# Two-layer MoE decoder on one core: the router worked out by token halves, and the gather by pieces

## The chip, the cores and the metric

The kernel runs on one core of a Trainium2 chip. The metric is the device time of one execution in microseconds (us), measured outside the profiler: 1168.0 us is the median of three runs (1166.81, 1168.00 and 1169.35). Everything is float32. One hardware DMA queue, driven by SyncE (SP), brings in all weights. TensorE (PE), VectorE (DVE) and ScalarE (ACT) compute; GpSimd clears one tile at the start and does nothing more.

## The reference, cut to what matters

256 tokens of width 1024 go through two layers. Each layer is a mixer (retention and HGRN2 in the first; stick-breaking and differential attention in the second) with an output projection, and then a hierarchical mixture of experts: every token picks one group of four by its group logits, and in that group the two best of eight experts, so that two of 32 experts work on it.

```python
x = x + mix.astype(x.dtype)                 # mixer with its output projection
h = rms_norm(x, norm_ffn[l])                # one scale per token, one gain per column
g_logits = hf @ wg_r + bg_r                 # 4 groups
g_sel = argmax(g_logits);  p_g = softmax(g_logits)[g_sel]
e_in  = (hf @ we_r + be_r)[group g_sel]     # 8 experts of that group
top_v, top_i = top_k(e_in, 2)
gate = p_g * softmax(top_v)
a = silu(xb @ w_gate[e]) * (xb @ w_up[e]);  y = a @ w_down[e]
out = segment_sum(y_rows * gate)            # and x = x + out
```

Every layer reads the gate, up and down matrices of all 32 experts, 2 MB each, 96 of them.

## The kernel before, in words

**Weights and places.** A unit is one 2 MB matrix, 128 partitions by 4096 numbers. SBUF holds twelve places for units (`RING + WIDE`); the mixer's input blocks, its two output blocks and the experts' 96 units pass through them in a fixed order. SP issues each load as soon as the unit that lay in its place before has been used; the counter `unit_used` (raised by the last matmul that reads a unit) says so. Experts go by quads of four: the units of a quad are four gate matrices, four up, four down. While the mixer still runs, SP loads the first quad (units 0 to 11 of the layer) into places as they come free. The last two of these are held back: unit 5 goes to the place of the second output block, so it waits for the last matmul of the output projection; unit 6 lies where the turned tokens and the router's weights are, and waits for the router's `strips`. Unit 12 needs the place of unit 0, so it waits for the first expert matmuls. Unit 0 of the first quad is cut by rows (`QUARTERED`): units 0 to 3 hold rows 0 to 255, 256 to 511 and so on of all four gate matrices, so that after row chunks 0 and 1 (of eight) unit 0 is used up, after 2 and 3 unit 1, and so on. Units 16 to 83 come by fours in one transfer (`load_matrices`, L391).

**Output projection and router** (`project_out` L1109, `route_and_experts` L1140 on PE; `finish_mixer` on ACT L1364 and on DVE L1540; `route` L1582 on DVE). The tokens are two halves of 128. PE finishes half 0, then the first 512 columns of half 1, turns the eight blocks of x of half 0 (`turn_x`, 128 by 128 transposes), does two matmuls for the second 512 columns of half 1, turns four more blocks, and does the last two matmuls. The last of them raises `unit_used`. Then come the router's strips for half 0 (`strips`: eight matmuls of 64 rows, two chunks side by side in the array), the last four blocks of x, the strips of half 1 and the `logits` matmuls that add the two strips. DVE adds the mixer's sums into x, copies the strips of half 0, and works out the inverse root mean square of both halves after all squares (ACT makes Ln and Exp, DVE refines with four operations). Then `route` takes both halves at once: scores (L1602), 640 differences of pairs (L1605), their comparison (L1606), their sum (L1608), the chosen group (L1609), the picked experts (L1611). PE counts ranks (L1170 to L1174), DVE writes the rank table (L1617) and the selection matrix `sel` (slots of 32 tokens for each of four experts: a comparison, L793, and a multiplication with the tokens' scales, L799). PE gathers the tokens by matmuls with `sel` (L577), ACT multiplies by the gains on the way to `xT` (L743), and the gate matmuls (L631) begin with the first two chunks. Between these PE writes x into the sum banks (`start_sums`, L558) and does two filler matmuls (`keep_busy`, L553).

**The quads.** For each quad: gate, up, gather of the next quad, four transposes, down, spreading back. ACT makes the sigmoid, DVE the product. `lbt`, `consts` and the like are small tables.

**Order.** All of it is written out by hand: each engine runs its own list in order, and waits on counters. Nothing reorders it.

## Time and profile before

| what | value |
|---|---|
| median of three runs | 1168.0 us |
| the profiled execution's own time | 1166.55 us |
| its span | 1164.8 us |
| PE busy | 876.4 us (75%) |
| DVE busy | 223.8 us (19%) |
| ACT busy | 126.7 us (11%) |
| bytes moved | 447.45 MB, 384 GB/s on the mean |
| mean granted TensorE clock | 0.877 |

The page of the profile cuts the span into 40 slices of 29.1 us; a digit is a busy share in tenths. The router stages lie in slices 6 and 26, at about 157 to 183 us and 722 to 748 us. The view of windows gives busy times of the engines in stretches that one chooses, and last the granted clock, the share and the speed of the DMA engines. The timeline gives start, length, engine, line, operation, tiles and shapes, and behind "x" how many instructions are merged in a row; a float32 matmul is two instructions. "SPq" is SyncE's issue of a transfer, not the transfer.

### The profile page before, as it was taken

What the parts mean: (1) busy time and instruction counts of PE and PEld (TensorE: products, weight loads), DVE (VectorE), ACT (ScalarE), POOL (GpSimd) and SP (SyncE); (2) the same over time, 40 slices, a digit from 0 to 9 for tenths busy, and PEclk for the clock granted to TensorE, in tenths of its full rate; (3) what the DMA queues carried; (4) which work ended last, traced back from release to release, by engine and by line L of the source; (5) the groups of instructions that cost most, each with busy time, mean ns of one, the idle gap of its engine ahead of it and who ended that gap; (6) DMA issues with size and microseconds to landing.
All of it is one profiled execution on the core that took longest, in us unless ns stands there. A gap on an engine that the chain in (4) does not pass through costs nothing.

```text
span 1164.8 us, 11459 instructions
## 1 busy us (share of the span) xinstructions
PE 876.4 (75%) x5104; PEld 394.0 (34%) x5104; DVE 223.8 (19%) x470; ACT 126.7 (11%) x249; POOL 0.5 (0%) x5
## 2 busy tenths in 40 slices
PE   8999999747474738485899999977474747474776
PEld 7555554212121212121246655433131313131312
DVE  2732332010101010101127541410000101000001
ACT  3411311000000000000021431200000000000000
POOL 0000000000000000000000000000000000000000
PEclk9999999888888877777999999998787878788889
DMA  9776659999999999999996477899999999999997
GB/s 347 304 321 257 267 219 378 430 435 433 435 433 433 435 433 435 435 430 414 424 423 284 154 293 276 317 441 433 433 435 435 433 435 433 433 430 432 417 426 308
DMA packets 19637, 447.45 MB, mean 384 GB/s; under 512 B 2560, under 2 KB 2816, under 8 KB 5504
## 3 DMA queue, kind: packets, MB, share of 16 engines
q1 hardware_dynamic: 19584, 446.67, 91.0%
q8 instruction: 43, 0.70, 0.2%
q14 instruction: 10, 0.08, 0.0%
HBM read 445.61 MB, written 1.05 MB: 383 GB/s over the span
## 4 chain that ended last, share of the span: by engine, by line
DMA 56%; PE 42%; DVE 1%; another core or an unknown queue 1%; issue 0%; ACT 0%; SPq 0%; DVEq 0%
DMA places<-in_together 47%; PE psum L631 14%; PE psum L1016 11%; DMA places<-in_quarters 8%; PE psum L1117 5%; PE psum L1013 4%; PE psum L577 1%; PE psum L1029 1%; PE psum L1057 1%; PE psum L565 1%; DMA places<-in_w_in 0%; PE psum L1144 0%; PE psum L698 0%; PE psum L968 0%
## 5 line engine op out<-in xcount | busy, mean ns | idle before, releaser
L631 PE MATMUL psum<-places,mixed 128*32 128x512 f32 x3040 | 421.8, 707 | 276.3 <-DMA places<-in_together 249.2
L631 PEld LDWEIGHTS psum<-places,mixed 128*32 128x32 f32 x3040 | 110.4, 127 | 570.5 <-issue 448.7
L1016 PE MATMUL psum<-places 128*128 128x512 f32 x288 | 126.3, 593 | 0.0
L1016 PEld LDWEIGHTS psum<-places 128*128 128x128 f32 x288 | 53.6, 190 | 61.4 <-issue 61.2
L577 PEld LDWEIGHTS psum<-sel,x 128*128 128x128 f32 x528 | 60.4, 192 | 17.0 <-issue 15.1
L577 PE MATMUL psum<-sel,x 128*128 128x128 f32 x528 | 64.3, 279 | 1.7 <-DVE sel L799 1.7
L565 PE MATMUL psum<-y_sb,spread 128*128 128x512 f32 x128 | 59.6, 606 | 2.1 <-ACT y_sb L768 1.4
L820 DVE TENSOR_TENSOR sig<-psum,sig 128x512 f32<-128x512 f32 x16 | 11.1, 692 | 253.4 <-ACT sig L760 253.4
L823 DVE TENSOR_TENSOR mixed<-psum,sig 128x512 f32<-128x512 f32 x16 | 11.1, 692 | 245.4 <-PE psum L631 245.4
L833 DVE COPY y_sb<-psum 128x512 f32<-128x512 f32 x14 | 9.7, 692 | 180.2 <-PE psum L631 180.2
L762 ACT COPY mixed<-psum 128x512 f32<-128x512 f32 x16 | 9.4, 586 | 320.6 <-PE psum L675 320.6
L1013 PE MATMUL psum<-places 128*128 128x256 f32 x192 | 42.9, 381 | 0.0
L1013 PEld LDWEIGHTS psum<-places 128*128 128x128 f32 x192 | 36.1, 190 | 5.7 <-issue 1.0
L760 ACT ACTIVATE sig<-psum 128x512 f32<-128x512 f32 x16 | 9.6, 597 | 255.9 <-PE psum L631 255.9
L565 PEld LDWEIGHTS psum<-y_sb,spread 128*128 128x128 f32 x128 | 22.8, 189 | 38.6 <-issue 33.7
L768 ACT COPY y_sb<-psum 128x512 f32<-128x512 f32 x16 | 9.4, 586 | 209.2 <-PE psum L631 181.8
L1117 PE MATMUL psum<-places,y_sb 128*128 128x512 f32 x64 | 28.2, 594 | 0.7 <-ACT small L1396 0.7
L1117 PE MATMUL psum<-places 128*128 128x512 f32 x64 | 28.5, 592 | 0.0
L826 DVE TENSOR_TENSOR mixed<-psum,consts 128x512 f32<-128x512 f32 x32 | 21.9, 690 | 31.8 <-PE psum L577 31.8
L1117 PEld LDWEIGHTS psum<-places,y_sb 128*128 128x128 f32 x64 | 11.9, 190 | 14.8 <-issue 13.9
L1388 ACT ACTIVATE places<-psum,small 128x512 f32<-128x512 f32 x16 | 10.1, 684 | 57.7 <-PE psum L1016 53.6
L1117 PEld LDWEIGHTS psum<-places 128*128 128x128 f32 x64 | 11.8, 190 | 13.4 <-issue 13.4
(252 smaller groups left out, 505.4 us busy)
## 6 DMA issues: line engine op xcount, KB each, us to landing
places<-in_singles SPq DMA_DIRECT2D x32, 2048.0 KB, 10.1
places<-in_quarters SPq DMA_DIRECT2D x22, 2048.0 KB, 35.1
places<-in_w_in SPq DMA_DIRECT2D x12, 2048.0 KB, 26.7
places<-in_w_out SPq DMA_DIRECT2D x4, 2048.0 KB, 14.3
places<-in_quarters SPq DMA_DIRECT2D x4, 1024.0 KB, 45.6
places<-in_w_in SPq DMA_DIRECT2D x2, 1024.0 KB, 27.2
places<-in_w_in SPq DMA_DIRECT2D x3, 512.0 KB, 8.7
x<-in_x SPq DMA_DIRECT2D x2, 512.0 KB, 13.6
```

The lines of the kernel that those rows point to most:

```text
L565: mm = pe.matmul(psum[:, ACC + 2 * n + tc, :], spread[:, tc, :], y_sb[:, 512 * n:512 * (n + 1)], start=False, stop=False, skip_group_check ...
L577: mm = pe.matmul(psum[:, YB + c // 4 if bank is None else bank, (c % 4) * P:(c % 4 + 1) * P], x[:, tc, c * P:(c + 1) * P], sel[:, tc, :], ...
L631: mm = pe.matmul(psum[slots, out + n, :], inp[:, c, slots], slot(layer, unit)[:, at + 512 * n:at + 512 * (n + 1)], start=c == 0, stop=c == ...
L820: turn(nc.vector.tensor_tensor(sig, psum[:, GATE, :], sig, ALU.mult))
L823: nc.vector.tensor_tensor(flat(act_h), psum[:, UP, :], sig, ALU.mult).then_inc(m["act_ready"], 1)
L826: nc.vector.tensor_tensor(xT[:, 4 * half:4 * half + 4, :], psum[:, 6 + half, :].rearrange("p (c s) -> p c s", s=P), gain_cols[:, 2 + layer ...
L1013: mm = pe.matmul(banks[:, m // 2, (m % 2) * SEQ:(m % 2 + 1) * SEQ], w[:, c, m * P:(m + 1) * P], hT[:, c, :], start=c == 0, stop=c == KC - 1)
L1016: mm = pe.matmul(banks[:, m, :], hT[:, c, m * P:(m + 1) * P], w[:, c, :], start=c == 0, stop=c == KC - 1)
L1029: mm = pe.matmul(psum[:, 4 + m, 0:SEQ], w[:, c, m * P:(m + 1) * P], hT[:, c, :], start=c == 0, stop=c == KC - 1)
L1057: mm = pe.matmul(banks[:, m, :], hT[:, c, m * P:(m + 1) * P], w[:, c, :], start=c == 0, stop=c == KC - 1)
L1117: return pe.matmul(psum[:, OUT_BANK[layer] + 2 * tc + n, :], mixT(half)[:, c, tc * P:(tc + 1) * P], w[:, c, 512 * n:512 * (n + 1)], start= ...
L1388: r = nc.scalar.activation(dst[:, tc * 512:(tc + 1) * 512], proj(g)[:, tc, :], function, scale=small[:, 2 + tc:3 + tc])
```

## The change

The diff computes the same in another order and in smaller pieces.

- `project_out` takes in the strips of half 0 ahead of the last-but-one output matmul, and the logits of half 0 ahead of the last one.
- Each half has a root of its own (`ask_root`, `refine_root`, `mean_square`); ACT takes the first after the turned half 0 is copied.
- `route` works by half: scores, differences, picks and ranks of half 0, then of half 1. The addition of the last 512 columns to x (`finish_x`) stands behind the differences of half 0.
- `sel` is 0 or 1 without the scales. The scale of each slot comes from one narrow matmul (`scale_slots`) and a copy by ACT (`keep_scale`), and enters in the sigmoid, in the product with it and in that with the up result, for every quad.
- The first gather goes by chunks: one, one, two, two, two, each between gate matmuls (`begin_gather`, `go_on_gathering`); the counts for the overflow test come in the midst of it. The gate values' exponentials and the load of the sigmoid's table come behind the gather, `start_sums` for three of four banks between the gate and the up matrices, and the read of the count into PE's register after the last gate matrix.

```diff
-ROOTS = ((2, 2), (20, 8), (28, 8), (2, 2), (2, 2), (44, 16), (44, 16), (44, 8), (2, 2))
+ROOTS = ((2, 2), (20, 8), (28, 8), (2, 1), (3, 1), (2, 2), (44, 16), (44, 16), (44, 8), (2, 1), (3, 1))
...
+            def scale_slots(bank):
+                for tc in range(TC):
+                    mm = pe.matmul(psum[:, bank, SEQ:SEQ + 1], sel[:, tc, :], small[:, 2 + tc:3 + tc], start=tc == 0, stop=tc == TC - 1)
+                return mm
+            def begin_gather():
+                pe.wait_ge(S["sel_first"], layer + 1)
+                gather_some(0, 1, YB + 1, (0,))
+                gather_some(1, 2, YB, (0,))
+                pe.wait_ge(m["sel_ready"], 1)
+                gather_some(0, 1, YB + 1, (1,)).then_inc(S["gather_begun"], 1)
+                gather_some(1, 2, YB, (1,))
+                scale_slots(YB).then_inc(S["gather_begun"], 1)
+            def go_on_gathering(c):
+                begun = 3 * layer
+                if c == 0:
+                    pe.wait_ge(S["xT_begun"], begun + 1)
+                elif c == 1:
+                    pe.wait_ge(S["xT_begun"], begun + 2)
+                elif c == 2:
+                    gather_some(2, 4, YB + 1, range(TC)).then_inc(m["gathered"], 1)
+                    count_picked(pe)
+                    pe.wait_ge(m["xT_ready"], 1)
+                elif c == 3:
+                    gather_some(4, 6, YB, range(TC)).then_inc(S["gather_begun"], 1)
+                elif c == 4:
+                    pe.wait_ge(S["xT_begun"], begun + 3)
+                elif c == 5:
+                    gather_some(6, 8, YB + 1, range(TC)).then_inc(m["gathered"], 1)
+                elif c == 6:
+                    pe.wait_ge(m["xT_ready"], 2)
...
                 if first:
-                    pe.wait_ge(S["xT_begun"], layer + 1)
+                    matrix(0, 0, GATE, xT, KC, FF, each_chunk=go_on_gathering)
+                    start_sums(pe, layer, (1, 2, 3))
+                    pe.wait_ge(S["route_ready"], layer + 1)
...
-                nc.scalar.activation(sig, psum[:, GATE, :], ACT.Sigmoid).then_inc(m["sig_ready"], 1)
+                nc.scalar.activation(sig, psum[:, GATE, :], ACT.Sigmoid, scale=slot_scale).then_inc(m["sig_ready"], 1)
...
             def one_hots(quad):
-                placed(sel, quad)
-                nc.vector.tensor_tensor(sel, sel, small[:, 2:4].unsqueeze(2).broadcast_to([P, TC, P]),
-                                        ALU.mult).then_inc(m["sel_ready"], 1)
+                placed(sel, quad).then_inc(m["sel_ready"], 1)
...
                         turn_x(pe, layer, 1, 0)
-                        for c in range(2, 4):
-                            mm = out(1, c, 1)
+                        pe.wait_ge(S["router_ready"], layer + 1)
+                        pe.wait_ge(S["xT_first"], layer + 1)
+                        strips(layer, 0, range(KC)).then_inc(S["strips"], 1)
+                        out(1, 2, 1)
+                        pe.wait_ge(S["strips_kept"], layer + 1)
+                        logits(0).then_inc(S["logits_done"], 1)
+                        mm = out(1, 3, 1)
                     mm.then_inc(S["unit_used"], 1)
...
+                pe.wait_ge(S["xT_second"], layer + 1)
+                strips(layer, 1, range(KC // 2))
                 turn_x(pe, layer, 1, 1)
                 pe.wait_ge(S["xT_third"], layer + 1)
-                strips(1, range(KC // 2, KC)).then_inc(S["strips"], 1)
-                start_sums(pe, layer, (0,))
+                strips(layer, 1, range(KC // 2, KC)).then_inc(S["strips"], 1)
                 pe.wait_ge(S["last_strips_kept"], layer + 1)
                 logits(1).then_inc(S["logits_done"], 1)
-                start_sums(pe, layer, (1, 2, 3)).then_inc(S["sums_started"], 1)
-                keep_busy(pe, 2, 7, ident, consts[:, 0:SEQ])
+                pe.wait_ge(S["picked_ready"], TC * layer + 1)
+                pe.matmul(psum[:, 4, 0:32], before, picked[:, 0, :], start=True, stop=True).then_inc(S["ranks_done"], 1)
+                start_sums(pe, layer, (0,))
+                pe.wait_ge(S["scores_read"], layer + 1)
+                pe.matmul(psum[:, 5, 0:32], ones[:, 0:P], picked[:, 0, :], start=True, stop=False)
+                keep_busy(pe, 2, 7, ident, consts[:, 0:SEQ])
+                pe.wait_ge(S["picked_ready"], TC * layer + 2)
+                pe.matmul(psum[:, 5, 0:32], before, picked[:, 1, :], start=False, stop=True).then_inc(S["ranks_done"], 1)
...
+                dve.wait_ge(S["squares"], SQUARES[2 * layer] + 2)
+                scores(0)
+                differences(0)
+                finish_x(layer)
+                pick(0)
+                dve.wait_ge(S["squares"], SQUARES[2 * layer + 1])
+                turn(V.tensor_tensor(small[:, 1:2], small[:, 1:2], small[:, 7:8], ALU.add))
+                ask_root(mean_square(dve, layer, 1), 3, 1)
+                refine_root(dve, turn)
+                scores(1)
+                V.memset(small[:, 60:61], 0.0).then_inc(S["scores_read"], 1)
+                differences(1)
+                pick(1)
+                place_first(0).then_inc(S["sel_first"], 1)
+                place_first(1).then_inc(M[layer]["sel_ready"], 1)
```

## Rows read from the trace of the kernel before

**Rows 1.** The page: DMA share by slice, GB/s by slice, and the chain's shares.
```profile
DMA  9776659999999999999996477899999999999997
GB/s 347 304 321 257 267 219 378 430 435 433 435 433 433 435 433 435 435 430 414 424 423 284 154 293 276 317 441 433 433 435 435 433 435 433 433 430 432 417 426 308
...
DMA 56%; PE 42%; DVE 1%; another core or an unknown queue 1%; issue 0%; ACT 0%; SPq 0%; DVEq 0%
```

**Rows 2.** Windows around both routers; the last column is GB/s.
```profile
156.50:164.50 8.00, 8.00 (x30) 3.90 (x28) 1.99 (x4) 3.37 (x6) 0.00 (x0) 1.00 0.00 0
164.60:176.50 11.90, 10.93 (x80) 7.60 (x84) 7.94 (x27) 2.51 (x8) 0.00 (x0) 1.00 0.90 352
176.50:179.00 2.50, 2.50 (x23) 1.06 (x23) 1.46 (x9) 2.10 (x5) 0.00 (x0) 1.00 0.02 7
179.00:184.00 5.00, 5.00 (x49) 2.35 (x51) 2.03 (x6) 1.15 (x4) 0.00 (x0) 1.00 0.95 331
729.70:741.30 11.60, 10.62 (x75) 7.41 (x76) 7.94 (x27) 2.38 (x8) 0.00 (x0) 1.00 0.92 362
743.60:754.00 10.40, 10.40 (x96) 4.33 (x100) 3.20 (x10) 1.96 (x6) 0.00 (x0) 1.00 0.91 356
```

**Rows 3.** Timeline of SP's issues: units 5, 12, 16 to 19; layer 1: 5, 12.
```profile
164.59 0.33 SPq L369 DMA_DIRECT2D places<-in_singles  x1
...
178.42 0.33 SPq L369 DMA_DIRECT2D places<-in_singles  x1
...
192.63 0.33 SPq L391 DMA_DIRECT2D places<-in_together  x1
...
729.73 0.33 SPq L369 DMA_DIRECT2D places<-in_singles  x1
...
743.57 0.33 SPq L369 DMA_DIRECT2D places<-in_singles  x1
```

**Rows 4.** Timeline of the first router, from the output projection's end to the sums.
```profile
160.72 1.01 ACT L974 COPY places<-psum 128x1024 f32<-128x1024 f32 x1 [1.90 <-PE psum L968]
...
162.67 1.88 PE L1117 MATMUL psum<-places 128*128 128x512 f32 x4
...
164.49 1.09 PE L1144 MATMUL psum<-places 128*64 128x128 f32 x16
164.59 0.69 DVE L1551 TENSOR_TENSOR x<-x,psum 128x512 f32<-128x512 f32 x1 [4.06 <-PE psum L1117]
...
166.69 0.21 ACT L866 ACTIVATE small<-small 128x2 f32<-128x2 f32 x1
...
168.58 0.31 PE L1149 MATMUL psum<-both_strips,mixed 128*128 128x40 f32 x2
...
168.72 2.82 PE L558 MATMUL psum<-x,consts 128*128 128x512 f32 x6
```

**Rows 5.** The same timeline, from the pairs to the first gate matmuls.
```profile
169.46 0.82 DVE L1605 TENSOR_TENSOR mixed<-mixed 128x640 f32<-128x640 f32 x1
...
172.03 0.17 DVE L1609 TENSOR_SCALAR mixed<-mixed 128x8 f32<-128x8 f32 x1
172.24 0.23 DVE L1611 SCALAR_TENSOR_TENSOR picked<-mixed 128x64 f32<-128x64 f32 x1
...
172.52 0.43 PE L1170 MATMUL psum<-picked,consts 128*128 128x64 f32 x2
...
173.97 0.42 DVE L799 TENSOR_TENSOR sel<-sel,small 128x256 f32<-128x256 f32 x1
...
174.45 2.05 PE L577 MATMUL psum<-sel,x 128*128 128x128 f32 x16 [0.86 <-DVE sel L799]
...
175.65 0.63 ACT L743 ACTIVATE mixed<-psum,consts 128x128 f32<-128x128 f32 x2 [7.65 <-PE psum L577]
...
176.44 1.92 PE L631 MATMUL psum<-places,mixed 128*32 128x512 f32 x16
...
177.38 1.28 ACT L1383 ACT_TABLE_LOAD   x1
```

More of the change, by code:

```diff
@@ L711, in moe_pe @@
             y_all = 2 * QUADS
+            count = pe.value_load(over_i[0:1, layer:layer + 1], min_val=0, max_val=SEQ)
             with pe.If(count > SLOTS):
@@ L771, in act_quad @@
                     nc.scalar.copy(y_sb[:, 512:1024], psum[:, YB + 1, :]).then_inc(m["y_ready"], 1)
-            keep_gathered(n17 + 1, first=not over)
+            if over:
+                keep_gathered(n17 + 1)
+            else:
+                begin_gathered()
             with act.Fori(0, QUADS if over else QUADS - 1) as i:
@@ L1107, in turn_half, with strips, logits @@
                 turn_mixed(pe, layer, half)
+            def strips(layer, tc, chunks):
+                for c in chunks:
+                    at = 64 * (c % 2)
+                    mm = pe.matmul(psum[at:at + 64, 4 + tc, 0:P], rw[layer][:, c, :], hT[:, c, tc * P:(tc + 1) * P],
+                                   start=c < 2, stop=c >= KC - 2)
+                return mm
+            def logits(tc):
+                return pe.matmul(psum[:, 4 + tc, SEQ:SEQ + SCORES], by_logit[:, tc * P:(tc + 1) * P], both_strips,
+                                 start=True, stop=True)
             def project_out(layer, meanwhile):
@@ L1640, in gates @@
                 V.tensor_reduce(rt[:, 8:10], differ, AX, ALU.add).then_inc(S["top_diff"], 1)
+                largest_count(layer)
                 dve.wait_ge(S["group_exp"], layer + 1)
```

204 lines of the change are left out of this document (101 added, 103 removed).

## The prediction

> **What bounds the kernel now.** I read the page first. Its slices show two kinds of stretch [rows 1]: the expert stages run at 430 to 435 GB/s with the DMA share at 9 for 13 or so slices each, and the mixers (slices 0 to 5, 21 to 25) move 154 to 347 GB/s. The chain gives 56% to DMA and 42% to PE [rows 1]. So the mixers go at PE's pace, the expert stages at the transfers' pace, and a stage with experts ends a fixed number of bytes after its stream starts: what moves that start moves the end by as much, twice in the kernel.
>
> So I looked next, by windows, at where the stream really starts. From 156.5 to 164.5 nothing moves [rows 2], since all free places are filled. At 164.59 SP issues unit 5, the release being the last output matmul; unit 6 follows behind the strips, while 5 is under way [rows 3]. From 164.6 to 176.5 the two are moved: 11.9 x 352 = 4.19 MB, which is 9.7 us at 433 GB/s. They were over by about 176.1 (11.6 x 362 = 4.20 MB by 741.3 in layer 1), so an issue into an idle queue costs 176.1 - 164.6 - 9.7 = 1.8 us before the stream counts as full. Then comes a hole: 7 GB/s from 176.5 to 179.0 [rows 2]. Unit 12 is issued at 178.42 [rows 3], when row chunks 0 and 1 of the gate are done. From 179 to 184 only 5 x 331 = 1.66 MB move, 3.8 us at full speed, so the stream counts as full from 180.2, again 1.8 us after the issue. The hole is worth 180.2 - 176.1 = 4.1 us. In layer 1 the issue is at 743.57 and 10.4 x 356 = 3.70 MB are 8.55 us of full speed by 754.0: full from 745.45, unit 6 over at 741.2, hole 4.2 us.
>
> Two events set the start of the endless stream, then: A, the release of unit 5 (the last output matmul), after which 11.5 us of transfer follow; and B, the release of unit 12 (gate chunk 1). Before, B is the late one. Full speed from then on is the later of A + 11.5 and B + 1.8. The change pulls B ahead and pushes A back.
>
> **A, the output projection's tail.** Strips of half 0 are 16 instructions, 1.09 us with the array's run-out and 1.02 from start to start; logits two instructions, 0.31 us [rows 4]. Both now stand ahead of the last output matmul. Strips wait for the copy of turned half 0, done at 160.72 + 1.01 = 161.73 [rows 4], and PE gets to them at 162.84 (the start of the last four output instructions, 162.67, plus array time): no wait. Then an output matmul of two instructions (4 take 1.72 us between starts, so 0.86) to 164.72. Logits need DVE's copy of the strips (128 wide; 0.29 us by the fixed part and slope worked out below), which stands behind the root: ACT's Ln and Exp (0.21 each [rows 4]) after the copy, 161.73 + 0.45, then four dependent small operations of 0.17 with 0.04 between them [rows 5], to 163.0. Strips end at 163.86, the copy at 164.2, half a microsecond ahead of need. So A moves by 1.02 + 0.35 = 1.4 us, to 166.0. If the root came later than that, it would delay A one for one (rival 3). Unit 6 needs the strips of half 1, now at about 169.1; unit 5 is under way until 172.6, so this is hidden. A + 11.5 = 177.5.
>
> **B, the chain to the second gate chunk.** DVE, in order: scores of half 0 at 165.2; differences of 320 instead of 640 elements. 640 cost 0.82 and 64 cost 0.23 [rows 5], a slope of 1.02 ns and a fixed 0.16, so 320 cost 0.49. By the slope alone it would be 0.33, by the whole row 0.82, and I keep these as ends. To 165.95. Then the addition to x, 0.69 us [rows 4], after A, to 166.75. Picks of half 0: 0.49 + 0.49 + 0.17 + 0.20 and gaps: to 168.25. ACT's squares of the last 512 columns end at 167.6, so the second root starts at 168.25: sum, mean, Ln, Exp, four refinements, some 1.7 us: 169.95. Beside it PE turns the last four blocks once x is added (166.95 to 167.5), ACT copies them to 168.25 behind its squares, PE does four strips to 169.05, ACT keeps them to 169.4, logits stand at 169.95. Both arms meet; scores of half 1 at 170.0. Then 0.21, a marker of 0.1, 0.49, 0.49, 0.49, 0.17, 0.20 with gaps: picked at 172.35. Before it was 172.24 + 0.23 = 172.47 [rows 5]: the splitting by itself gives next to nothing here, because A moved and each fixed cost is paid twice.
>
> What is won comes after. Ranks are one matmul instead of four (0.43 for two instructions [rows 5], the others were beside); rank table and `sel` of half 0 (0.20 + 0.29) run while PE does the ranks of half 1; then 0.20 + 0.29 for half 1, and no multiplication of `sel` (0.42 [rows 5]): `sel` ready at 173.55 against 173.97 + 0.42 = 174.4. Next PE needs two more gather instructions before ACT may start, not eight: 16 take 2.05 [rows 5], so 0.26 for 2; with the handover of 0.15 seen before ACT's row (eight at 174.45 + 0.99, ACT at 175.65), ACT starts at 174.0. One chunk costs it 0.31 (half of 0.63 [rows 5]), PE begins the gate at 174.45 where it was 176.44, and chunk 1 is ready before chunk 0 ends (0.86 to 0.93, an eighth of the 16 instructions' 1.92 by fours [rows 5]). B = 174.45 + 2 x 0.87 = 176.2, where it was 178.42: 2.2 us earlier. B + 1.8 = 178.0.
>
> **The sum for one layer.** Full speed from the later of 177.5 and 178.0, before 180.2: 2.2 us. But at 176.2 the queue is still busy with unit 6, and an issue into a busy queue may be spared part of the 1.8 us; the trace shows no such late join, so between 0 and 0.5 us more. I take 0.2: 2.4 us a layer, bounds 2.2 and 2.7. Layer 1 has the same order and nearly the same times from A on (13.84 us from A to B against 13.83 [rows 3]): 4.8 us for both.
>
> The 1.8 us are read from the front of a transfer: 7 GB/s until 179.0, 0.6 us after the issue, then 331 GB/s over five microseconds [rows 2]. The Trainium skill says otherwise: its page "DMA: Bandwidth & Descriptors", section "Anatomy of one DMA — SWDGE (gpsimd) path", puts most of a fixed cost of about 2 us behind the last byte, as the write's receipt. What that would make of the time is rival (2); the rows do not bear it out for this queue.
>
> **What else is moved.** The remaining gathers now stand between gate chunks: two chunks' gather 0.99 and counting 0.4 ahead of chunk 2, and ACT's two chunks: chunk 3 ends at 180.9, which releases unit 13. Unit 12 lasts to 178.0 + 4.84 = 182.8; an issue is wanted 1.8 before that, at 181.0. It just fits. The gate ends at 185.5. Then three sums, 6 instructions, 2.6 us of PE (2.82 with run-out [rows 4]), which were formerly under DVE's picking, and up's 6.9: the up units are used at 195.1 where it was 192.63 [rows 3]. Units 12 to 15 last until 178.0 + 19.35 = 197.35; wanted by 195.55. It fits by 0.5 us. If that cover is gone, each microsecond of PE costs one. ACT's exponentials and table load (some 1.7 us) now end at about 185.3, beside the gate; the weights of `selw` are wanted 10 us later. The read of the count before the branch in the last quad stands where PE waits for transfers anyway. In each of the 16 quads there come four narrow matmul instructions and a small copy (0.6 us together by the 0.17 and 0.43 us rows), and 0.42 of DVE goes. The three products with an added per-slot scalar keep their 512 elements; ends are no change and 0.1 us each. All of this lies where PE waits for transfers, and 0.6 us before the last quad's down matrix, whose last quarters come some 12 us later. I count 0.
>
> **The time.** The profiled execution took 1166.55 with a span of 1164.8; minus 4.8 it would be 1161.75 and 1160.0. It lies 1.45 under the median, so for the median 1168.0 - 4.8 = 1163.2 us.
>
> **Rivals.** (1) The sums and gathers that moved behind the gate eat the cover of 0.5 us: if up's release is 1.5 us later than worked out, the first transfer of four comes 1.0 too late in each layer: 1165.2. For it: three separate PE to ACT handovers in the gate. Against it: those rows are all short.
> (2) The slow start is no lost time, made up by the sixteen engines later: then the hole is only 176.1 to 178.5 (unit 12's issue), and after the change full speed runs from 177.5, a gain of 1.0 us a layer: 1166.0. For it: 433 GB/s is a mean over units in flight together. Against it: the 331 GB/s. It is what would follow from the page named above.
> (3) Slower: the hold of the output projection. Unit 5 is queued behind PE's wait for the copied strips, that behind DVE's root, that behind ACT's Ln and Exp. It costs from the first 0.5 us of lateness on and turns the gain into a loss when A moves by more than 180.2 - 11.5 - 164.6 = 4.1 us, that is when logits stand 2.7 us later than worked out. One load of an activation table there (1.28 us [rows 5]) would make A + 2.2, still faster. With logits 3.6 us late, as when ACT's pair is served only after the squares and the copies of half 1 (some 4 us of its list), it is A + 5.0: 1168.0 + 2 x 0.9 = 1169.8. For it: three engines in a ring at a place where before there was no wait. Against it: ACT is free from 161.73 on.
> (4) B comes late, because the second half's chain on DVE (18 dependent operations) costs 0.1 more at each: B = 178.0, 0.4 a layer, 1167.2.
>
> **How the numbers follow.** Forecast 0.58, with its own range 1161.5 to 1164.8 (bounds 2.2 and 2.7 a layer, give or take 1.2 us of the median seen in three runs); (1) 0.14; (2) 0.06; (3) 0.09; (4) 0.13. 0.2% is 2.3 us, about what a measurement of this kernel can tell from no change. Faster takes the forecast, (1) but for a few hundredths, and a share of (2) and (4): 0.57 + 0.11 + 0.04 = 0.72. Same: the rest of those, 0.19. Slower: (3), 0.09. The range is 1160.8 to 1167.6.
>
> **What would show it.** In the profile after: unit 5's issue 3.1 us after the strips' start, where it stood at their start; unit 12's issue 10.2 us behind unit 5's, not 13.8; no window near 0 GB/s between unit 6 and unit 12, nor before the first transfer of four. The forecast is wrong if a hole remains, if logits of half 0 wait for DVE, or if the first transfer of four is issued into an empty queue.

## The result, and the profile after

| | median us | range us | runs |
|---|---|---|---|
| before | 1168.07 | 1166.41 to 1169.35 | 18 |
| after | 1170.62 | 1167.13 to 1172.03 | 18 |

The ratio is 1.0018, 95% interval 1.0011 to 1.0026: some 2 us slower, where 4.8 us faster was forecast. The profiled execution of after took 1171.11 us with a span of 1169.3 (before: 1166.55 and 1164.8) at the same mean granted clock of 0.877. PE's program grew from 5104 matmul records to 5180.

The page of after, against [rows 1]: DMA and GB/s by slice, the queue that brings instructions, the chain's shares. In the slices of the experts nothing is gained. The instruction queue moved 45 packets (before: 43 and 0.70 MB). PE's share of the chain rose by 3 points, and "issue" from 0% to 1%.

```profile
DMA  9776659999999999999996476899999999999996
GB/s 346 301 284 275 254 194 421 431 431 435 431 431 433 431 435 431 435 433 411 424 422 279 154 295 271 335 446 433 430 434 430 434 437 432 430 435 433 415 425 266
...
q8 instruction: 45, 0.74, 0.3%
...
DMA 51%; PE 45%; another core or an unknown queue 1%; DVE 1%; issue 1%; ACT 1%; SPq 0%; DVEq 0%
```

SP's issues of units 5, 12 and 13 and the first transfer of four, against [rows 3]:

```profile
168.83 0.33 SPq L370 DMA_DIRECT2D places<-in_singles  x1
...
178.91 0.33 SPq L370 DMA_DIRECT2D places<-in_singles  x1
...
183.87 0.33 SPq L370 DMA_DIRECT2D places<-in_singles  x1
...
198.38 0.33 SPq L392 DMA_DIRECT2D places<-in_together  x1
```

All of this stands 2.8 us late, for a reason that has nothing to do with the change: the first projection took 16.87 us in this execution and 14.05 in that of before (last section). So from here on times are also given from a mark. "From unit 4" is the distance from unit 4's issue, which stands at 149.54 in before and 152.34 in after; "from the output block" is the distance from the issue of layer 1's output block (611.15 and 613.60).

| from unit 4's issue | before | after | moved | forecast |
|---|---|---|---|---|
| A: unit 5 issued | 15.05 | 16.49 | +1.44 | +1.4 |
| B: unit 12 issued | 28.88 | 26.57 | -2.31 | -2.2 |
| unit 13 issued | 32.72 | 31.53 | -1.19 | just in time |
| first transfer of four issued | 43.09 | 46.04 | +2.95 | just in time |
| layer 1's output block issued | 461.61 | 461.26 | -0.35 | -2.4 |

Layer 1, from the output block: A 118.58 to 120.02, B 132.42 to 130.10, unit 13 136.26 to 135.06, the first transfer of four 146.64 to 149.57. The last copy of the kernel starts at 550.47 before, 552.57 after: +2.10.

Windows over after's router, against [rows 2]; the last column is GB/s. The hole of 7 GB/s is gone, as forecast. In its place come six microseconds at 339.

```profile
176.50:179.00 2.50, 2.50 (x24) 1.04 (x23) 0.75 (x4) 0.76 (x3) 0.00 (x0) 1.00 0.99 426
179.00:181.00 2.00, 1.65 (x16) 1.35 (x19) 0.34 (x2) 0.63 (x2) 0.00 (x0) 1.00 1.06 369
181.00:184.00 3.00, 3.00 (x28) 1.36 (x24) 0.00 (x0) 0.63 (x2) 0.00 (x0) 1.00 0.86 339
184.00:187.00 3.00, 3.00 (x29) 1.36 (x25) 0.33 (x2) 1.19 (x5) 0.00 (x0) 1.00 0.89 339
187.00:190.00 3.00, 3.00 (x20) 1.12 (x13) 2.75 (x12) 1.59 (x2) 0.00 (x0) 1.00 0.97 388
```

The timeline of the router (start, length, engine, line, operation, tiles, shapes; "x" counts merged instructions), against [rows 4, 5]:

```profile
165.57 1.09 PE L1171 MATMUL psum<-places 128*64 128x128 f32 x16
...
168.27 0.49 DVE L1675 TENSOR_TENSOR mixed<-mixed 128x320 f32<-128x320 f32 x1
...
174.68 0.19 DVE L1686 SCALAR_TENSOR_TENSOR picked<-mixed 128x32 f32<-128x32 f32 x1
...
175.60 0.29 DVE L1693 TENSOR_TENSOR sel<-consts,rank 128x128 f32<-128x128 f32 x1
...
176.93 1.92 PE L668 MATMUL psum<-places,mixed 128*32 128x512 f32 x16
```

Less 2.8, `picked` is ready at 172.07 (forecast 172.35), `sel` at 173.09 (173.55), the gate begins at 174.13 (174.45). The router does what was said of it.

The last quad of layer 1 does not do what was said of it. PE's matmuls of its up matrices (the first two rows) and of its down matrices in after:

```profile
1133.69 1.07 PE L668 MATMUL psum<-places,mixed 128*32 128x512 f32 x8 [0.34 <-issue]
1139.56 7.55 PE L668 MATMUL psum<-places,mixed 128*32 128x512 f32 x56 [4.81 <-issue]
1150.28 1.92 PE L668 MATMUL psum<-places,mixed 128*32 128x512 f32 x16 [1.01 <-ACT spread L814]
1153.63 1.92 PE L668 MATMUL psum<-places,mixed 128*32 128x512 f32 x16
1156.97 1.92 PE L668 MATMUL psum<-places,mixed 128*32 128x512 f32 x16
1158.71 1.04 PE L732 MATMUL psum<-places,mixed 128*32 128x512 f32 x8
...
1166.17 0.69 DVE L892 COPY x<-psum 128x512 f32<-128x512 f32 x1 [0.17 <-PE psum L566]
```

and in before (up matrices, again the first two rows, then the first of the down matrices, and the end):

```profile
1129.94 5.36 PE L631 MATMUL psum<-places,mixed 128*32 128x512 f32 x48
1136.98 1.92 PE L631 MATMUL psum<-places,mixed 128*32 128x512 f32 x16 [1.68 <-DMA places<-in_quarters]
1141.97 1.92 PE L631 MATMUL psum<-places,mixed 128*32 128x512 f32 x16 [1.30 <-DMA places<-in_quarters]
...
1154.14 1.07 PE L698 MATMUL psum<-places,mixed 128*32 128x512 f32 x8 [0.53 <-DMA places<-in_quarters]
...
1161.62 0.69 DVE L845 COPY x<-psum 128x512 f32<-128x512 f32 x1 [0.17 <-PE psum L565]
```

Before, PE waits for each of the quarters, and last for the first half of the last unit (the row at 1154.14). After, it stands for 4.81 us after eight instructions, waiting for nothing that the profile names, and then never waits for a transfer again: it is itself what ends last. Two windows of after show that it pays twice, since the granted clock (the column before DMA's share) is 0.50, the level of 1.2 GHz, in the 2.5 us after it has stood:

```profile
1133.60:1139.50 5.90, 1.07 (x8) 0.27 (x9) 0.00 (x0) 0.00 (x0) 0.00 (x0) 0.95 1.03 436
1139.50:1142.00 2.50, 2.44 (x12) 0.69 (x15) 0.00 (x0) 0.00 (x0) 0.00 (x0) 0.50 1.00 426
```

So the forecast failed in two places: the stream lost what the router had won, and layer 1's end got a stall of its own. The experiments take them one by one.

### The profile page after: what moved, and what is told of

Same layout as the page of the kernel before. It is cut to its first block, busy times and chain, and to the rows that moved or that the text cites. A ratio compares the mean times of both kernels' runs of the same rounds, so it can differ in the third digit from the quotient of the medians.

```text
span 1169.3 us, 11671 instructions
## 1 busy us (share of the span) xinstructions
PE 886.6 (76%) x5180; PEld 405.3 (35%) x5180; DVE 221.7 (19%) x478; ACT 130.3 (11%) x271; POOL 0.5 (0%) x5
## 4 chain that ended last, share of the span: by engine, by line
DMA 51%; PE 45%; another core or an unknown queue 1%; DVE 1%; issue 1%; ACT 1%; SPq 0%; DVEq 0%
DMA places<-in_together 43%; PE psum L668 15%; PE psum L1075 11%; PE psum L1187 5%; DMA places<-in_singles 4%; DMA places<-in_quarters 4%; PE psum L1072 4%; PE psum L583 2%; PE psum L1088 1%; PE psum L1116 1%; PE psum L566 1%; PE psum L559 0%; DMA places<-in_w_in 0%; PE psum L732 0%
## 5 line engine op out<-in xcount | busy, mean ns | idle before, releaser
L1075 PEld LDWEIGHTS psum<-places 128*128 128x128 f32 x288 | 53.6, 190 | 61.4 <-issue 61.2
L870 DVE SCALAR_TENSOR_TENSOR mixed<-psum,slot_scale,sig 128x512 f32<-128x512 f32 x16 | 12.0, 750 | 245.7 <-PE psum L668 245.7
L867 DVE SCALAR_TENSOR_TENSOR sig<-psum,slot_scale,sig 128x512 f32<-128x512 f32 x16 | 12.0, 750 | 241.9 <-ACT sig L810 241.9
L1072 PE MATMUL psum<-places 128*128 128x256 f32 x192 | 42.9, 381 | 0.0
L1072 PEld LDWEIGHTS psum<-places 128*128 128x128 f32 x192 | 36.1, 190 | 5.7 <-issue 1.0
L810 ACT ACTIVATE sig<-psum,slot_scale 128x512 f32<-128x512 f32 x16 | 11.0, 687 | 239.2 <-PE psum L668 239.2
L1088 PE MATMUL psum<-places 128*128 128x256 f32 x64 | 16.9, 433 | 1.9 <-DMA places<-in_w_in 1.9
```

Of the source, the lines that this page charges most:

```text
L810: nc.scalar.activation(sig, psum[:, GATE, :], ACT.Sigmoid, scale=slot_scale).then_inc(m["sig_ready"], 1)
L867: turn(nc.vector.scalar_tensor_tensor(sig, psum[:, GATE, :], slot_scale, sig, ALU.mult, ALU.mult))
L870: nc.vector.scalar_tensor_tensor(flat(act_h), psum[:, UP, :], slot_scale, sig, ALU.mult, ALU.mult).then_inc(m["act_ready"], 1)
L1072: mm = pe.matmul(banks[:, m // 2, (m % 2) * SEQ:(m % 2 + 1) * SEQ], w[:, c, m * P:(m + 1) * P], hT[:, c, :], start=c == 0, stop=c == KC - 1)
L1075: mm = pe.matmul(banks[:, m, :], hT[:, c, m * P:(m + 1) * P], w[:, c, :], start=c == 0, stop=c == KC - 1)
L1088: mm = pe.matmul(psum[:, 4 + m, 0:SEQ], w[:, c, m * P:(m + 1) * P], hT[:, c, :], start=c == 0, stop=c == KC - 1)
```

## The experiments

One theory for the stand was that the count is now read into PE's register at a late place; the other, put in numbers with e4, that it comes from the place of the instructions in PE's program. A second pair, for the stream: whether the stream loses its lead at unit 13's join or at the first transfer of four. All ratios are to the kernel before, with the 95% interval. "Behind the branch" counts PE's matmul records.

### The count read early (e1)

```diff
                     start_sums(pe, layer, (1, 2, 3))
                     pe.wait_ge(S["route_ready"], layer + 1)
+                    counts.append(pe.value_load(over_i[0:1, layer:layer + 1], min_val=0, max_val=SEQ))
...
-            count = pe.value_load(over_i[0:1, layer:layer + 1], min_val=0, max_val=SEQ)
+            count = counts[0]
```

> The kernel after, with one edit: PE reads the count of the fullest expert into its register after the first gate matrix and the sums, not right ahead of the branch in the last quad. In the profile after, PE stood 4.81 us in the second layer's last quad (1.02 in the first's) a few matmuls behind that branch, with nothing waited for, and the last down quarter was reached at 1158.7 where its data were due by about 1156.9. Theory 1 (the late read puts PE's instruction supply on the path): the stall goes in both layers, the end is bound by transfers again, and the time falls by 1.8 to 2.8 us, to about 1168.3. Rival (the stall belongs to the branch itself or to chance, and the lost time lies in the stream of transfers): the stall stays or the time stays within 0.5 us of the kernel after, about 1170.6.

1169.13 us, 1.0010 (1.0000 to 1.0019). The time fits neither forecast, 1168.3 nor 1170.6, and the interval overlaps that of after. The stand of layer 1 is there: 4.56 us after nine instructions. Where the count is read has nothing to do with it. It has to do with a small one of layer 0, ahead of the first matmul behind the branch: 1.02 us in after, 0.46 to 1.04 in all nine kernels that read the count late, and none in before, b2 and e1, which read it early. The transfers hide it: after still waits 0.57 us for the next one.

### The sums and the counts moved (e2, e3)

e2 writes the sum banks 0 and 1 during the picking and 2 and 3 after the first up matrices; e3 moves the counting matmuls from chunk 2 of the first gate to chunk 6 as well.

```diff
-                    start_sums(pe, layer, (1, 2, 3))
...
+                if not over and i == 0:
+                    start_sums(pe, layer, (2, 3))
...
-                start_sums(pe, layer, (0,))
+                start_sums(pe, layer, (0, 1))
...
-                keep_busy(pe, 2, 7, ident, consts[:, 0:SEQ])
```
```diff
-                    count_picked(pe)
                     pe.wait_ge(m["xT_ready"], 1)
...
                 elif c == 6:
+                    count_picked(pe)
                     pe.wait_ge(m["xT_ready"], 2)
```

> The kernel after, with x written into the sum banks at other places: banks 0 and 1 during the picking (the two filler matmuls go), banks 2 and 3 behind the first up matrix, none between gate and up. Theory 2a (up's release is too late for the transfers by four): first transfer of four issued 2.6 us earlier against unit 12's issue, the stream's lead after it stays at 0.6 to 0.8 us a layer instead of falling to 0.3 (0.35 us won in layer 0 at the end, 0.3 lost in layer 1), time 1169.2 to 1169.8. Theory 2b (the lead is lost before, when unit 13 joins the queue): the first transfer of four comes earlier, and the landing of the last quarters does not: within 0.4 us of the kernel after.

> As e2_sums_moved, and the two matmuls that count the picks stand behind gate chunk 5, not ahead of chunk 2. So unit 1 of the quad is used up 0.4 us sooner and unit 13 is issued 4.5 instead of 4.9 us behind unit 12. In the kernel after the stream led the one of before by 2.0 us when unit 12 had joined and by 0.8 when unit 13 had. Theory 2b (each join needs an issue some 2.8 us ahead of the predecessor's end, not 1.8 as predicted): 0.3 to 0.4 us a layer of lead come back, 0.6 to 0.8 us in all against e2. Rival (the 1.8 us of the prediction are right and the loss is of the array of engines at unit 12's join alone): no change against e2.

e2: 1169.91, 1.0012 (1.0002 to 1.0021). e3: 1168.93, 1.0016 (1.0005 to 1.0026). Neither interval can be told from after's, and e2's time lies between its two forecasts. e2's first transfer of four is issued at 43.13 from unit 4, as early as before's, yet its lead over before at 203 is 0.15 us, the same as after's (the table under e5 tells how the lead is counted), which speaks for theory 2b. e3 was no test of 2b: unit 13 came 4.95 us behind unit 12 in both layers, as in after, and not 4.5 as expected. e3 issues the first transfer of four at 44.99 from unit 4, where after has 46.04, yet layer 1's output block comes only 0.2 us earlier (461.06). At this mark b1 and b2 (below), whose layer 0 has before's router, stand at 461.50 and 462.22, so a few tenths there aren't clear of chance. The 0.5 us of cover that the prediction worried about (its rival 1) was therefore not the main loss. Both stand at the end, for 4.13 and 3.81 us.

### The kernel before, with the count read late (b1)

```diff
-                count = pe.value_load(over_i[0:1, layer:layer + 1], min_val=0, max_val=SEQ)
...
+            count = pe.value_load(over_i[0:1, layer:layer + 1], min_val=0, max_val=SEQ)
```

> The kernel before, with one edit: PE reads the count right ahead of the branch in the last quad, as the kernel after does, instead of after the first gather. Theory 1: PE stands for some microseconds behind the branch in the last quads; in layer 1 that puts it on the path, 0.5 to 2.8 us slower than before, 1168.6 to 1170.9. Rival: no stall, the time of before within 0.4 us.

1168.19, 1.0002 (0.9993 to 1.0011). From the output block to the last copy 550.69, against 550.47: the late read costs at most 0.2 us. With e1 that rules out the count as the cause of layer 1's stand.

### The same matmuls at other places of the program (e4, b2)

```diff
+                if not over and i in range(3, 3 + 1):
+                    for _ in range((0, 15)[layer]):
+                        pe.matmul(psum[:, GATE, 0:16], ident, consts[:, 0:16], start=True, stop=True, skip_group_check=True)
```

(b2: `range(3, 3 + 4)` and `(0, 12)[layer]`.)

> The kernel after with 15 tiny matmuls (16 columns, 60 engine instructions, some 1.5 us of PE) into a free bank ahead of the fourth quad's gate in layer 1, where PE waits for transfers for 5 us and more. They compute nothing that is used. What has been seen: the stall in the last quad's up matrix (4.81, 4.56, 4.13 and 3.81 us) came 8, 9, 16 and 16 matmul instructions behind the branch in the kernel after and in e1, e2, e3. Counting a weight load and a matmul for each and four for each float32 matmul call, PE's program reaches the branch's taken side at instruction 12434, 12432, 12418 and 12418, so the stall always comes at the same count modulo 256: 12434 + 16 = 12432 + 18 = 12418 + 32 = 12450. In the kernel before the taken side starts at 12238, which is 212 instructions from the next such place, and no stall was seen. Theory 3 (a block of PE's program that begins right behind the branch isn't there in time): the stall goes from the last quad, the end is bound by transfers as before, 2.0 to 3.0 us less than the kernel after: 1167.6 to 1168.6. Rival (it is the new gathers and sums that make the end PE's): stall and time stay, about 1170.6.

> The kernel before with 48 such tiny matmuls, 12 ahead of each of four quads' gates in layer 1 (1.2 us of PE each, in waits of 5 us), so that the branch's taken side starts at the kernel after's place modulo 256 (142 against 146). Nothing of the router is changed. Theory 3: a stall of 3.8 to 4.8 us about 10 matmul instructions into the last up matrix of layer 1, and 1.5 to 3 us more than before: 1169.6 to 1171. Rival: as before, 1168.1.

The last quad of e4, then of b2:

```profile
1131.57 5.36 PE L668 MATMUL psum<-places,mixed 128*32 128x512 f32 x48 [0.52 <-issue]
```
```profile
1130.45 1.91 PE L631 MATMUL psum<-places,mixed 128*32 128x512 f32 x10
1136.51 8.90 PE L631 MATMUL psum<-places,mixed 128*32 128x512 f32 x54 [4.15 <-issue]
```

After lost its stand and before got one, after ten instructions as counted. From the output block to the last copy e4 takes 550.87 (after: 552.57, so 1.70 less) and b2 552.32 (before: 550.47, so 1.85 more). The medians go the same way, by less than was expected: e4 1168.85, 1.0007 (0.9996 to 1.0018), some 1.3 us under after by the ratios where 2.0 to 3.0 were forecast, and its interval reaches after's 1.0018; b2 1169.09, under the forecast 1169.6 to 1171, but 1.0015 (1.0006 to 1.0023) is clear of 1. The code of the change isn't what stalls; its length is. What a stand costs at the end is worked out below, behind e8, since these two differences also hold what the transfers did.

### All moved: the gather later too (e5)

e3, with the gather of chunks 4 and 5 moved from ahead of gate chunk 3 to ahead of chunk 4, so that unit 1's last use comes earlier and unit 13 is issued 3.73 us behind unit 12 instead of 4.96; and 19 small matmuls, which again give 212.

```diff
-                elif c == 3:
-                    gather_some(4, 6, YB, range(TC)).then_inc(S["gather_begun"], 1)
                 elif c == 4:
+                    gather_some(4, 6, YB, range(TC)).then_inc(S["gather_begun"], 1)
                     pe.wait_ge(S["xT_begun"], begun + 3)
```

> e3 with two more edits: chunks 4 and 5 are gathered ahead of gate chunk 4, not ahead of chunk 3, so that unit 1 is used up another 1.0 us sooner; and 19 tiny matmuls in layer 1's fourth quad put the branch at the place of the kernel before modulo 256. Theory 2b (an issue is wanted about 3 us ahead of its predecessor's end, so unit 13 comes too late): unit 13 is issued some 3.6 us behind unit 12 (4.9 in the kernel after); the stream's lead over before, once unit 13 runs, is 1.4 us or more a layer instead of 0.8; with the stall gone the time is 1165.6 to 1166.6. Rival (the joins are not what costs): lead 0.8 at most, time 1167 or more.

1166.65 us (lowest and highest 1164.86 and 1167.36), 0.9986 (0.9977 to 0.9995): it beats both kernels. The issues of units 12 and 13 and the windows of e5, which stand 3.0 us ahead of those of after:

```profile
175.92 0.33 SPq L370 DMA_DIRECT2D places<-in_singles  x1
179.65 0.33 SPq L370 DMA_DIRECT2D places<-in_singles  x1
```
```profile
178.00:181.00 3.00, 2.68 (x24) 1.23 (x16) 0.00 (x0) 0.28 (x2) 0.00 (x0) 1.00 0.86 339
181.00:184.00 3.00, 2.60 (x24) 1.28 (x24) 0.00 (x0) 0.76 (x4) 0.00 (x0) 1.00 0.98 415
184.00:187.00 3.00, 3.00 (x32) 1.20 (x28) 1.58 (x10) 1.69 (x4) 0.00 (x0) 1.00 1.02 437
```

The first answers to after's 181 to 184, the same 339 GB/s; the next two run at 415 and 437 where after has 339 and 388. I added up the bytes since unit 5's issue and divided the lead over before by 433 GB/s (times of before's scale):

| lead over before, us | at 182 | at 185 | at 191 | at 203 |
|---|---|---|---|---|
| after | 1.74 | 0.87 | 0.66 | 0.15 |
| e5 | 1.89 | 1.70 | 1.57 | 1.66 |

Layer 1 shows the same: after has 1.95 at 746 and 0.85 at 752, e5 about 1.8 at both. The other profiles, counted in the same way, bear it out. At 754 in layer 1 the five kernels that issue unit 13 4.95 us behind unit 12 (after, e1 to e4) lead by 0.66 to 0.81, and the three that issue it 3.73 us behind (e5, e7 and e8) by 1.80 to 1.87. In layer 0, at 191, it is 0.47 to 0.81 against 1.57 and 1.53; e7, whose unit 12 came 1.17 us late there, has 0.98. So half of the lead is lost at unit 13's join, because it was issued too late.

### The tail as before (e6)

e4, with strips and logits of half 0 behind the last output matmul again.

```diff
-                        strips(layer, 0, range(KC)).then_inc(S["strips"], 1)
                         out(1, 2, 1)
-                        logits(0).then_inc(S["logits_done"], 1)
                         mm = out(1, 3, 1)
...
+                strips(layer, 0, range(KC)).then_inc(S["strips"], 1)
+                logits(0).then_inc(S["logits_done"], 1)
                 pe.wait_ge(S["xT_second"], layer + 1)
```

> e4 with the output projection's end as in the kernel before: strips and logits of half 0 behind the last output matmul. Everything else as after. By the prediction's sum A is 1.4 us earlier and B, which hangs on the addition of the last columns, may come up to 1.4 us earlier or, since the scores of half 0 come later, stay. If A's shift is what eats the gain: 1 to 2 us less than e4. If B and the joins decide: within 0.5 us of e4.

1173.43, 1.0049 (1.0034 to 1.0064), the slowest of all, and outside both forecasts. Unit 5 comes 1.44 earlier (A 15.05), but unit 12 at 30.27, against 26.57 in after; layer 1's output block at 464.77, against 461.51 in e4. In DVE's list the addition of the last columns to x stands behind the differences of half 0, and these wait for logits that now come only after the last output matmul. That puts the addition at 17.84 from unit 4 (e4: 16.57), 1.27 of the 3.70 us. So most of the 1.44 us that the change gives away at A are what its order of DVE's list needs. The other 2.4 us go with the clock, which in this profile fell ahead of the first gather:

```profile
172.00:175.00 3.00, 2.63 (x10) 1.69 (x7) 2.08 (x9) 0.28 (x2) 0.00 (x0) 0.50 0.86 251
175.00:178.00 3.00, 3.00 (x10) 2.24 (x9) 1.11 (x5) 0.00 (x0) 0.00 (x0) 0.53 0.99 426
```

e4 has 1.00 there. In layer 1 the clock fell to 0.50 in e6 as well, and unit 12 came 2.4 us later than in e4. How much of the median is the clock's was not tried.

### Without the small matmuls, and with more (e7, e8)

e7 is e5 without them. e8 is e5 with three times as many, 19 in each of quads 3 to 5: a distance of 60, or 30 matmul instructions.

```diff
-                if not over and i in range(3, 3 + 1):
+                if not over and i in range(3, 3 + 3):
```

> Kernel e5_all_moved_padded without its 19 small matmuls in quad 3 of layer 1: the matmuls of the last quad stand where they stood in e3_sums_counts_moved, 32 instructions ahead of the place at which PE stood still (a place that was the same in four kernels, counted in steps of 256 instructions). In those four the still stand ended 5.9 us after the branch: 1.07 us for 8 instructions and 4.81 in the kernel after, about 2.1 for 16 and 3.81 in e3. Theory block (the standing is a fetch of instructions that begins at the branch): a stand of 3.8 us after 16 matmul instructions, and the end 1.7 to 1.9 us later than e5 measured from the issue of layer 1's first output block: 1168.4. Rival: the gather that moved from chunk 3 to chunk 4, not the padding, made e5 quick: then 1166.7 here and no stand.

> Kernel e5_all_moved_padded with 57 small matmuls (19 in each of quads 3, 4 and 5 of layer 1) instead of 19 in quad 3. The place lies 30 matmul instructions behind the branch (e5: 106, e3: 16, after: 8). Theory block with a fixed arrival 5.9 us after the branch: 30 instructions take 30 x 0.134 = 4.0 us, so PE stands still for 1.9 us (1.5 to 2.3) there; the cost of the whole is 0.5 to 1.2 us over e5: 1167.5. Rival A: the stand is always of some 4 us wherever the place is near the branch (a fetch that begins only when the place is reached): 1168.4. Rival B: no stand at all, since only the places within 16 of the branch are hit: 1166.7.

The last quad of e7, then of e8:

```profile
1129.05 1.93 PE L667 MATMUL psum<-places,mixed 128*32 128x512 f32 x16 [0.41 <-issue]
1135.56 7.86 PE L667 MATMUL psum<-places,mixed 128*32 128x512 f32 x48 [4.58 <-issue]
```
```profile
1129.54 3.63 PE L667 MATMUL psum<-places,mixed 128*32 128x512 f32 x30 [0.51 <-issue]
1135.14 4.45 PE L667 MATMUL psum<-places,mixed 128*32 128x512 f32 x34 [1.97 <-issue]
```

Thirty instructions and 1.97 us, where 1.9 was expected: that is the block theory with a nearly fixed arrival. Over the seven profiles with a stand PE goes on 5.6 to 6.5 us after its first matmul behind the branch. Its rivals (always 4 us, or none) fall. In e7 the stand is 4.58 rather than 3.8, after 16 as expected. From the output block to the last copy e5 takes 549.68, e8 550.45 (+0.77), e7 551.02 (+1.34). In the medians this is too small to tell: e7 1167.16, 0.9992 (0.9982 to 1.0001); e8 1167.11, 0.9990 (0.9981 to 0.9999). The forecast of 1168.4 for e7 was too high by 1.2, so the better stream does more for e5's time than the missing stand: by the ratios e3 to e7 (the gather moved) is 2.8 us, e7 to e5 (the stand gone) 0.7.

What a stand costs at the end can be told from the transfers. In each of the six profiles without one or with one that costs nothing (before, b1, e4, e5, e6 and e8) the last copy starts 7.52 us after the first half of the last unit has landed. What is more than that is PE's. Times from the output block:

| | half landed | last copy | between | PE's |
|---|---|---|---|---|
| before | 542.95 | 550.47 | 7.52 | 0 |
| after | 543.17 | 552.57 | 9.40 | 1.88 |
| e1 | 543.72 | 553.42 | 9.70 | 2.18 |
| e2 | 543.61 | 552.29 | 8.68 | 1.16 |
| e3 | 543.29 | 551.51 | 8.22 | 0.70 |
| e4 | 543.35 | 550.87 | 7.52 | 0 |
| b2 | 544.47 | 552.32 | 7.85 | 0.33 |
| e5 | 542.16 | 549.68 | 7.52 | 0 |
| e7 | 542.43 | 551.02 | 8.59 | 1.07 |
| e8 | 542.93 | 550.45 | 7.52 | 0 |

So after's stand cost 1.88 us. e8's cost nothing, since PE still waits for each quarter afterwards; its +0.77 over e5 is that of its transfers, and of b2's +1.85 in the profile 1.52 are. For b2 it is the median that shows the cost.

The instruction queue's own packets, of 16 KB each, agree. By windows of 0.2 us they stand in after at 1131.0 and 1136.8, and PE starts at 1133.69 and 1139.56; in e7 at 1126.4 and 1132.8, and PE starts at 1129.05 and 1135.56; in e8 at 1126.8 and 1132.8, with 1129.54 and 1135.14. The next block is fetched 5.8 to 6.4 us behind the first, and PE goes on 2.3 to 2.8 us after each packet's window. Before has them too, at 1127.2 and 1133.0, but needs the second only after 106 instructions. Why the second fetch comes so long behind the first was not tried.

The Trainium skill, page "Runtime: NRT & Kernel Launch", section "Instruction fetch mechanics", says that instructions come in blocks of 256 (16 KiB) ahead of use, in sequence, and that a taken branch to a place outside the window breaks this. The traces agree, in the 16 KB of a packet and the step of 256; that crossing a block is "mostly hidden" holds here except at the first crossing behind the branch, where it comes 8 to 30 matmul instructions behind it; at 106 it is hidden too.

## Why the prediction was wrong, by its steps

The signs that it named did not warn: no hole remained, unit 5 was issued 3.26 us after the strips' start (3.1 forecast), unit 12 10.08 behind unit 5 (10.2), and the first transfer of four at 198.38 while unit 15 was under way.

- **What bounds the kernel.** Right in the main. It held the expert stages to the end to be the transfers' alone; for layer 1's last quad that is true only while PE has some 5 us to spare, and the change took them.
- **A, +1.4 and B, -2.2.** Right: +1.44 and -2.31, and in layer 1 +1.44 and -2.32. The picking and `sel` came within 0.5 us, a pair operation of 320 took 0.49 as taken from slope and fixed part, and no ring of PE, DVE and ACT held the projection (rival 3).
- **Full speed from B + 1.8, 2.2 to 2.7 us a layer.** Failed first here. The lead was 1.74 us at 182, and 1.95 in layer 1: joining a busy queue did not spare any of the 1.8, and the ramp stayed (369, then 339 GB/s).
- **"An issue is wanted 1.8 before", unit 13 "just fits".** The step that failed for the stream. 1.8 us was read from an issue into an empty queue and used as the lead that a following one needs. By the prediction's count unit 12 is over at 182.8, and after's unit 13 was issued at 149.54 + 31.53 = 181.1, 1.7 us ahead of that; the stream then ran at 339 and 388 GB/s and lost 1.74 - 0.66 = 1.1 us. In e5 it was issued at 149.54 + 30.29 = 179.8, 3.0 ahead, and 1.89 - 1.57 = 0.3 were lost. The lead wanted, ahead of that counted end, lies above 1.7 and near 3.0. It is no lead ahead of the landing: unit 12 landed 35.95 from unit 4 in both, that is 4.4 and 5.7 us behind those two issues. Nor is it a rule that holds to a tenth: in layer 0 of e3 unit 12 was 1.17 us late, unit 13 again 1.7 ahead by this count, and 1.25 - 0.81 = 0.4 were lost.
- **The first transfer of four.** Sized at 195.1, or 45.56 from unit 4; it came at 46.04, 0.5 late. The lead in layer 0 then fell from 0.66 to 0.15, but so it did in e2, to the same 0.15, with that issue at 43.13; and the transfer landed 19.34 us behind unit 15 in before and after alike. In layer 1 it landed 20.83 behind in after (before: 19.34), but 19.68 and 19.57 in e1 and e4, which issue it at the same time. So rival 1's mechanism is shown for 0.2 to 0.3 us in layer 1 at most.
- **"The read of the count ... stands where PE waits anyway", and the last quad counted at 0.** The read is harmless (e1, b1). But the prediction asked only what each new instruction takes, never what its being there does to those behind it in the program. The 4.81 us stand, and 2.5 us at the lower clock behind it, cost 1.88 us at the end of after; e4 loses the stand, and b2 gets one, without any change in the router.
- **Rivals.** Of the four none was it. (2), with 1.0 a layer, is near the lead that after kept at 185, but not for its reason: e5 shows the rest can be had by an earlier issue.

The sum from the two profiles, against before: the start +2.81 (no part of the change), layer 0 -0.35, layer 1 up to the last gate unit of its last quad +0.27 (506.27 to 506.55 from the output block, where PE starts on it), the end +1.82: +4.55 us, where the last copies start 1166.17 - 1161.62 = 4.55 apart. Without the start it is +1.74, and the medians' ratio says 0.0018 x 1168 = 2.1. The -0.35 and +0.27 lie within the scatter of like code: at the first mark b1 and b2 have 461.50 and 462.22 where before has 461.61, and at the second that unit lands at 506.50 in after and at 505.43 in e4, which differ only in the small matmuls.

**Open.** e5's lead of 1.9 us at 225 is sometimes 0.8 and sometimes 2.0 later on (from unit 4: 246.23 to 245.40, then 286.52 to 284.56), and of 2.0 us at the start of the last quad's last gate unit (506.27 to 504.26) only 0.79 are left at the first half of the last unit (542.99 to 542.20). e8 keeps 0.01. All twelve profiles have late landings of this kind. In before the transfer at 286.39 from unit 4 lands 20.85 us behind the one ahead of it, where 19.34 is usual, and in e5 the one at 245.35 comes 20.43 behind. The places differ from run to run, and the sum hardly does: from the landing of unit 15 to that of the last mixer input block ahead of layer 1's output block it is 421.9 to 422.8 us in all twelve. At its end e5 leads before by 1.94, though at the landing of layer 0's last unit, and at the output block's issue, it led by only 0.73. So the lead was there, and the places of the late landings hid part of it. The windows of e5 at the end show one:

```profile
1151.10:1153.10 2.00, 1.50 (x16) 0.16 (x8) 0.00 (x0) 0.00 (x0) 0.00 (x0) 1.00 0.46 193
1153.10:1155.10 2.00, 1.29 (x6) 0.49 (x3) 0.00 (x0) 0.59 (x1) 0.00 (x0) 1.00 0.04 16
```

The second has four packets of 8 KB, one after the other, 0.3 us each: one of the sixteen engines is behind the others, and a transfer is over only with its last piece. Which engine, and why, was not tried.

## What to carry to other kernels

When a hole in a stream of transfers is closed, the next issues become the late ones: check each of them with a lead well above the time that an empty queue takes to start, here near 3 us ahead of the counted end rather than 1.8. When code is added ahead of a branch, the matmuls behind it move in the instruction blocks; if the next block begins fewer than about 45 matmul instructions behind a taken branch (an estimate, 5.9 us by 0.134; measured are stands at 8 to 30 and none at 106), PE stands, and a few harmless instructions ahead of it move the place. It costs only what it takes beyond the time that PE has to spare: nothing in e8, 1.88 us in after. And compare two profiles from marks near each part, never by absolute times, since a chance difference at the start can be larger than the effect.

## What the runs showed of the hardware beyond that

The clock column prints 1.00 also where the trace has no clock record. The windows of the kernel start, before first and after second, with the same code:

```profile
9.00:12.00 3.00, 3.00 (x15) 2.64 (x15) 0.53 (x2) 0.58 (x3) 0.00 (x0) 1.00 1.02 403
```
```profile
9.00:12.00 3.00, 3.00 (x8) 2.37 (x7) 0.62 (x2) 0.89 (x3) 0.00 (x0) 1.00 1.00 395
```

Eight matmuls instead of fifteen in three microseconds, both at 1.00, and the start was 2.8 us longer; over the twelve profiles, unit 4's issue came between 149.34 and 152.34. The trace's first clock record stands at 5.1 us in before and at 12.5 in after; up to there PE's matmuls come 0.4 us apart, from there on 0.2. So the slow stretch looks like the lower level of the clock, ahead of any record. At the router the clock is shown: in e7 it was 0.54 here, and two sums took 3.56 us where e5 at 1.00 took 1.96, which made its unit 12 1.17 us later.

```profile
168.00:171.00 3.00, 1.74 (x16) 1.26 (x16) 2.22 (x11) 1.86 (x6) 0.00 (x0) 1.00 0.87 262
171.00:174.30 3.30, 3.30 (x6) 1.33 (x6) 2.71 (x10) 0.00 (x0) 0.00 (x0) 0.54 1.00 427
```

Ahead of the fall PE was busy for 1.74 of 3.00 us; e5 had 1.74 of 3.00 at the same place and no fall, so the same schedule may or may not be hit. After's two filler matmuls stood there, which e2, e3, e5, e7 and e8 lack; of these five, the clock fell in e3 and e7. But it fell in e6 too, which has them, in both layers.

An added per-slot scalar makes DVE's product of 512 elements 750 ns instead of 692, and ACT's sigmoid with a scale tile 687 instead of 597 ns. Both stand where PE waits for transfers.
